# Recurrence computed two tiles at a time inside the input projection, output projection contracted in halves beside the attention norm

## What is computed

```python
proj = h @ W["w_in_even"][e]                      # 2048 -> 5120
q, k, v, xl, gl = jnp.split(proj, [...])          # 1024 columns each
q = rope(rmsnorm(q), pos); k = rope(rmsnorm(k), pos)
o = attn_prompt(q, k, v, lam)  or  attn_sample(q, k, v, k_past, v_past, lam)
o = rmsnorm(o, subln) * (1 - lam_init)            # the attention norm, per head
xc = causal_dwconv(xl, lru_buf, w, b)
r = sigmoid(einsum(xc, wa) + ba); i = sigmoid(einsum(xc, wx) + bx)   # gates, 16 blocks of 64x64
a = exp(-8 * r * softplus(-lam)); drive = sqrt(-expm1(2 log a)) * i * xc
h_t = a_t * h_(t-1) + drive_t                     # the recurrence, over the 1024 channels
yl = gelu(gl) * h
y = concatenate([o, yl]) @ W["w_out_even"][e]     # output projection, 2048 -> 2048
```

## Time and profile before

| | |
|---|---|
| median of 3 runs | 3342.11 us (3337.58 to 3343.0) |
| the profiled execution | 3340.85 us |
| its span, first to last instruction | 3339.1 us |
| TensorE busy | 3139.5 us, 94% of the span |
| VectorE, ScalarE, GpSimd busy | 46%, 32%, 1% |
| mean granted TensorE clock | 0.966 of full speed |
| HBM traffic | 617 MB read, 186 GB/s over the span |

### The profile page before, as it was taken

How to read it: one execution, slowest core, us unless ns; L and a number is a source line. 1 busy time by engine, 2 the same in 40 slices (tenths; PEclk the granted TensorE clock), 3 DMA queues, 4 the chain that set the end, 5 groups by cost and what they waited for, 6 DMA issues and landing times.

```text
span 3339.1 us, 56135 instructions
## 1 busy us (share of the span) xinstructions
PE 3139.5 (94%) x21283; PEld 2863.0 (86%) x21283; DVE 1520.1 (46%) x2024; ACT 1082.2 (32%) x1295; POOL 29.7 (1%) x55
## 2 busy tenths in 40 slices
PE   6899987877899999999999989999899999999998
PEld 2588863447889989989989989999899999999998
DVE  1534565345544433433434554445544444444443
ACT  1322233134333233333233243333343333332332
POOL 0000000100000000000000000000000000000000
PEclk9899997888999999999999989999999999999999
DMA  9777777963476576576566434444444444444443
GB/s 340 246 249 247 252 254 268 340 248 93 147 233 198 159 232 206 158 227 211 160 220 214 151 114 151 147 148 147 126 139 151 150 147 149 150 148 148 150 150 108
DMA packets 512217, 624.17 MB, mean 187 GB/s; under 512 B 22416, under 2 KB 408081, under 8 KB 511444
## 3 DMA queue, kind: packets, MB, share of 16 engines
q1 hardware_dynamic: 504576, 595.68, 55.7%
q0 software_dynamic: 6112, 22.84, 1.8%
q10 hardware_dynamic: 1430, 4.24, 0.4%
HBM read 617.13 MB, written 5.54 MB: 186 GB/s over the span
## 4 chain that ended last, share of the span: by engine, by line
PE 88%; DVE 4%; DMA 4%; ACT 2%; issue 1%; SPq 1%; DVEq 0%; POOL 0%; ACTq 0%; POOLq 0%
PE mm L1452 82%; PE aux L1452 5%; DMA wide_first<-in_ada_mix_w 2%; DMA wide_later<-in_ada_mix_w 2%; PE mm L1545 1%; DVE a_rr L1216 1%; SPq L364 1%; DVE l_g L1336 0%; PE aux L1716 0%; ACT tmp L623 0%; DVE a_qn L1219 0%; DVE p_s L1243 0%; DVE pj L1227 0%; DMA wide_later<-in_ada_mlp_w 0%; DVE rstd L913 0%
## 5 line engine op out<-in xcount | busy, mean ns | idle before, releaser
L859 DVE TENSOR_TENSOR w_lo<-raw,w_hi 128x1024 fp32r<-128x1024 f32 x752 | 919.9, 1225 | 1439.6 <-ACT w_hi L536 1437.9
L536 ACT ACTIVATE w_hi<-raw 128x1024 fp32r<-128x1024 f32 x752 | 795.0, 1058 | 1734.1 <-PE mm L1452 1733.9
L1452 PE MATMUL mm<-h_hi,w_hi 128*128 128x320 f32 x3712 | 1166.0, 314 | 53.0 <-DVE h_lo L955 32.3
L1452 PE MATMUL mm<-h_lo,w_hi 128*128 128x320 f32 x3712 | 1152.4, 310 | 0.0
L1452 PE MATMUL mm<-h_hi,w_lo 128*128 128x320 f32 x3712 | 1152.3, 310 | 0.0
L1452 PEld LDWEIGHTS mm<-h_hi,w_hi 128*128 128x128 f32 x3712 | 702.6, 189 | 145.6 <-issue 145.6
L1452 PE MATMUL mm<-u_hi,w_hi 128*128 128x320 f32 x2304 | 712.0, 309 | 0.0
L1452 PE MATMUL mm<-u_lo,w_hi 128*128 128x320 f32 x2304 | 711.9, 309 | 0.0
L1452 PE MATMUL mm<-u_hi,w_lo 128*128 128x320 f32 x2304 | 711.9, 309 | 0.0
L1452 PEld LDWEIGHTS mm<-h_lo,w_hi 128*128 128x128 f32 x3712 | 702.8, 189 | 0.0
L1452 PEld LDWEIGHTS mm<-h_hi,w_lo 128*128 128x128 f32 x3712 | 702.1, 189 | 0.0
(11 more groups left out here) (256 smaller groups left out, 1241.2 us busy)
## 6 DMA issues: line engine op xcount, KB each, us to landing
raw<-in_mlp_w SPq DMA_DIRECT2D x512, 512.0 KB, 3.6
narrow<-in_ada_mlp_w SPq DMA_DIRECT2D x256, 256.0 KB, 3.5
raw<-in_w_in_odd SPq DMA_DIRECT2D x96, 512.0 KB, 3.6
raw<-in_w_in_even SPq DMA_DIRECT2D x80, 512.0 KB, 6.6
wide_first<-in_ada_mix_w SPq DMA_DIRECT2D x64, 512.0 KB, 8.8
narrow<-in_ada_mix_w SPq DMA_DIRECT2D x128, 256.0 KB, 3.7
wide_later<-in_ada_mlp_w SPq DMA_DIRECT2D x64, 512.0 KB, 6.2
wide_later<-in_ada_mix_w SPq DMA_DIRECT2D x64, 512.0 KB, 10.6
```

The lines of the kernel that those rows point to most:

```text
L536: fn(w_hi[:, slot], raw[:, slot], ACT.Copy).then_inc(hi_ready, 1)
L859: v.tensor_tensor(w_lo[:, slot], raw[:, slot], w_hi[:, slot].bitcast(F32), ALU.subtract).then_inc(lo_ready, 1)
L1452: return nc.tensor.matmul(out, lhsT, rhs, start=first, stop=last)
```

## The change

The recurrence leaves its place ahead of the output projection. It is done two tiles at a time in the turns of the input projection: turn i of the four gets the gate matmuls of tiles 2i and 2i+1 (PE, after the second and the fourth chunk of the second pair), their tanh, exponential and root (ACT), and DVE does the recurrence of pair i in the middle of turn i+1. Convolution and gelu start one turn earlier. The buffers `l_a`, `l_m`, `l_d` hold two tiles instead of eight. The gate weights are loaded at the start. The output projection's first two pairs are computed in halves: both pairs contract first over the recurrence's blocks, with the head sums of the attention norm between those halves, then over the attention's. SP loads the weight chunks in that order, and ACT and DVE interleave the first eight splits with the attention norm.

```diff
-        l_a = at("l_a", RH + LT * TILE, [P, LT, T])
...
+        l_a = at("l_a", RM + 4 * TILE, [P, 2, T])
+        l_m = at("l_m", RM + 6 * TILE, [P, 2, T])
+        l_d = at("l_d", RM + 8 * TILE, [P, 2, T])
         wgate = at("wgate", RU + 16 * TILE, [P, 2, LT, P])
...
             load_quad(slab(W_IN, 0, 11 * COLS))
-            load_quad(slab(A["w_out_even"][0], 0, 0))
+            halves = [slab(A["w_out_even"][0], 0, j * COLS) for j in range(2)]
+            for s in (2, 3):
+                load(halves[0](s))
+            for s in (2, 3):
+                load(halves[1](s))
             sp.wait_ge(chunk_used, 80)
             with looped(sp, 4, GROUPS, {KW: 8}) as g:
                 ada_wide(wide_later, 1, g)
             with looped(sp, 0, 8, {KW: 8}) as g:
                 ada_wide(wide_later, 2, g)
-            matrix(A["w_out_even"][0], 8, 1)
+            for half in halves:
+                for s in (0, 1):
+                    load(half(s))
+            matrix(A["w_out_even"][0], 8, 2)
...
-            turns_with_ada(4)
...
+            turns_with_ada(3)
+            def gates(j):
+                i, m = j // 2, j % 2
+                act.wait_ge(l_gates, j + 1)
+                if i and not m:
+                    act.wait_ge(l_stage, i)
+                fn(l_a[:, m], aux[:, 0, 0:T], ACT.Tanh, scale=0.5, bias=hb[:, 0, j:j + 1])
+                fn(l_d[:, m], mm[:, 2, 0, 0:T], ACT.Tanh, scale=0.5, bias=hb[:, 1, j:j + 1]).then_inc(l_tr, 1)
+                act.wait_ge(l_tr, j + 1)
+                fn(l_m[:, m], l_a[:, m], ACT.Tanh, scale=hb[:, 2, j:j + 1], bias=hb[:, 2, j:j + 1]).then_inc(l_t, 1)
+                act.wait_ge(l_t, 2 * j + 1)
+                fn(l_a[:, m], l_a[:, m], ACT.Exp, scale=hb[:, 3, j:j + 1], bias=hb[:, 3, j:j + 1]).then_inc(l_t, 1)
+                if m:
+                    act.wait_ge(l_t, 2 * j + 2)
+                    fn(l_m[:, :, :], l_m[:, :, :], ACT.Sqrt).then_inc(l_root, 1)
+            for i in range(4):
+                split()
+                act.wait_ge(g_poly, i + 1)
+                fn(g_tmp[:, :, :], g_tmp[:, :, :], ACT.Tanh, scale=GELU_C).then_inc(g_tanh, 1)
+                split(2)
+                gates(2 * i)
+                ada_out()
+                split(2)
+                gates(2 * i + 1)
...
+            act.wait_ge(stored, 64)
+            act.wait_ge(y_val, 4)
+            mixed(2)
+            squared(0)
+            mixed(3)
+            squared(1)
+            act.wait_ge(wide_used, 8 * 24)
+            split(1)
+            rooted(0)
+            split(1)
+            for i in range(1, H):
+                if i + 1 < H:
+                    squared(i + 1)
+                rooted(i)
+                if i in (2, 4):
+                    split(1)
+                if i == 4:
+                    act.wait_ge(s_out, 1)
+                    act.wait_ge(o_ready, 4)
+                    mixed(0)
+            split(2)
+            act.wait_ge(o_ready, H)
             mixed(1)
-            for n in (2, 3):
...
+            split(2)
+            rounds(1)
...
-            def turn_with_ada(out0, out1, a, g, extra=()):
+            def turn_with_ada(out0, out1, a, g, extra=(), mid=None):
                 for n in range(4):
                     split(1)
                     if n < len(extra):
                         extra[n]()
                 out0()
+                if mid is not None:
...
-            def projections(kind, turns, first, group=None, extra=None):
+            starts = slice(SEQ, T, DS)
+            def recurrence(i):
+                for m in range(2):
+                    j = 2 * i + m
+                    dve.wait_ge(l_tr, j + 1)
+                    v.scalar_tensor_tensor(l_d[:, m, 0:SEQ], l_d[:, m, 0:SEQ], 1.0, xl_p[:, j, 3:3 + SEQ], ALU.add, ALU.mult)
+                    d_s = l_d[:, m, SEQ:T].rearrange("p (b q) -> p b q", b=NB)
+                    ins = v.scalar_tensor_tensor(d_s, d_s, 1.0, xl_s[:, j, :, 3:3 + DS], ALU.add, ALU.mult)
+                step(ins)
+                dve.wait_ge(l_t, 4 * i + 4)
+                step(v.tensor_tensor(l_b[:, :, :], l_a[:, :, starts], h0[:, 2 * i:2 * i + 2, :], ALU.mult))
+                dve.wait_ge(l_root, i + 1)
+                step(v.scalar_tensor_tensor(l_m[:, :, :], l_a[:, :, :], 1.0, l_m[:, :, :], ALU.add, ALU.mult))
+                settle()
+                step(v.scalar_tensor_tensor(l_d[:, :, :], l_d[:, :, :], 0.5, l_m[:, :, :], ALU.mult, ALU.mult))
+                step(v.memset(l_a[:, :, starts], 0.0))
+                settle()
+                step(v.tensor_tensor(l_d[:, :, starts], l_d[:, :, starts], l_b[:, :, :], ALU.add))
+                settle()
+                for m in range(2):
+                    ins = v.tensor_tensor_scan(l_m[:, m], l_a[:, m], l_d[:, m], 0.0, ALU.mult, ALU.add)
+                step(ins)
+                settle()
+                y = pj[:, 24 + 2 * i:26 + 2 * i, :]
+                v.scalar_tensor_tensor(y, y, 0.5, l_m[:, :, :], ALU.mult, ALU.mult).then_inc(y_val, 1)
+                v.tensor_copy(lstage[:, 2 * i:2 * i + 2, 27:28], l_m[:, :, SEQ - 1:SEQ])
+                v.tensor_copy(lstage[:, 2 * i:2 * i + 2, 28:36], l_m[:, :, SEQ + DS - 1:T:DS]).then_inc(l_stage, 1)
...
-            projections(project, 4, 4, (1, 0), conv_and_gelu)
+            for i in range(5):
+                a, g = (0, 11) if i == 0 else (1, i - 1)
+                turn_with_ada(lambda: project(0, 4 * i), lambda: project(1, 4 * i + 2), a, g,
+                              conv_and_gelu(i) if i < 4 else (), (lambda: recurrence(i - 1)) if i else None)
...
+            low(2, 1)
+            low(3, 2)
+            split(1)
+            scaled_head(0)
+            split(1)
+            dve.wait_ge(s_back, 1)
+            for n in range(4):
+                rows, cols = slice(4 * (n % 2), 4 * (n % 2) + 4), slice(SEQ + 32 * (n // 2), SEQ + 32 * (n // 2) + 32)
+                ins = v.tensor_scalar(pj[:, rows, cols], mm[:, 2, 0, P * n:P * n + P].rearrange("p (j t) -> p j t", j=4),
+                                      subln[:, 0:1], None, ALU.mult)
+            ins.then_inc(s_out, 1)
+            for i in range(1, H):
+                scaled_head(i)
+                if i in (2, 4):
+                    split(1)
+                if i == 5:
+                    low(0, 3)
+            split(2)
+            low(1, 4)
+            split(2)
+            step(v.memset(sq_sum[:, :, :], 0.0))
...
+            def half_pair(r, s):
+                slot = K.off % SLOTS
+                pe.wait_ge(lo_ready, K.now + 1)
+                pe.wait_ge(h_ready, 4 + (s + 2) % 4 + 1)
+                for kk in range(4):
+                    for m in range(2):
+                        out, cols = mm[:, r, m, 0:T], slice(P * m, P * m + P)
+                        k = 4 * s + kk
+                        mul(out, w_hi[:, slot, kk, cols], h_hi[:, k, :], k == KT // 2, False)
+                        mul(out, w_hi[:, slot, kk, cols], h_lo[:, k, :], False, False)
+                        ins = mul(out, w_lo[:, slot, kk, cols], h_hi[:, k, :], False, k == KT // 2 - 1)
+                ins.then_inc(chunk_used, 1)
+                K.up()
             def norm():
...
+            def gates(j):
+                pe.wait_ge(l_conv, j // 2 + 1)
+                if j:
+                    pe.wait_ge(l_tr, j)
+                for n in range(2):
+                    out = (aux[:, 0], mm[:, 2, 0])[n]
+                    mul(out[:, 0:SEQ], wgate[:, n, j, :], xl_p[:, j, 3:3 + SEQ], True, True)
+                    ins = mul(out[:, SEQ:T].rearrange("p (b q) -> p b q", b=NB), wgate[:, n, j, :],
+                              xl_s[:, j, :, 3:3 + DS], True, True)
+                ins.then_inc(l_gates, 1)
+            pe.wait_ge(gate_in, 64)
+            for i in range(4):
+                def after(s):
+                    if s in (1, 3):
+                        gates(2 * i + s // 2)
+                    if s == 2:
+                        fold()
...
+            def head_sums(*heads):
+                for i in heads:
+                    pe.wait_ge(o_sq, i + 1)
+                    if i >= 2:
+                        pe.wait_ge(o_root, i - 1)
+                    mul((mm[:, 2, 1], aux[:, 0])[i % 2][:, 0:SEQ], C("ones"), l_g[:, 0, i % 2, 0:SEQ], True, True
+                        ).then_inc(o_ms, 1)
+            head_sums(0, 1)
+            pe.wait_ge(pair_free, G.now + 2)
+            half_pair(0, 2)
+            head_sums(2)
+            half_pair(0, 3)
+            head_sums(3)
+            half_pair(1, 2)
+            head_sums(4, 5)
+            half_pair(1, 3)
+            head_sums(6, 7)
+            for r in range(2):
+                half_pair(r, 0)
+                half_pair(r, 1)
+                G.up()
```

161 lines of the change are left out of this document (43 added, 118 removed).

## The result

The changed kernel takes 3301.71 us (median, 3300.98 to 3312.18) where the kernel before took 3339.85 us on the same chip (3336.23 to 3343.0): a ratio of 0.9894, 95% interval 0.9881 to 0.9908. It is 38 us faster (31 to 40 by the interval).

What follows compares the result with a forecast made beforehand. TensorE, busy for 94% of the span, was taken to bound the kernel. From 3340.85 us, 11.7 was added for the projection and 36.2 taken off before the output projection: 3316 us, range 3308 to 3328.

Steps and rivals of the forecast that it cites:

- The projection: Input projection: eight tiles' gate matmuls at 1.46 us each on TensorE's path add 11.7 us (10.6 to 12.8).
- the room before the fold: Input projection: ScalarE's ares copy is done at +13.3, TensorE's fold arrives at +14.3, 1.0 us to spare.
- The stretch before the output projection: Recurrence leaves, norm interleaved with eight splits and half pairs: chunk 8 ends at 774.5 instead of 810.7, saving 36.2 us.
- The clock's share: Output projection's first eight chunks: two slow-clock restarts at 1.5 us and 0.3 for chunk 1.
- waits for sums: Beside the attention norm: 4.8 of VectorE's 34.2 us from 722.9 to 757.1 are waits for head sums.
- rival A: Beside the norm the clock stays low, a chunk costs 6.4 us: 3323.7 (first four) to 3335 (all eight); chance 0.16.
- Nothing elsewhere: After the first eight output-projection chunks: both kernels do the same 24 chunks, so nothing was counted there.
- 810.7 is the time to beat: Output projection: TensorE turns to the row transposes at 810.69 in the old kernel; the new end is compared with it.
- B: Input projection pays more: a tile costs 2.2 us and the fold waits 1 us in three turns: 3325; chance 0.10.
- C: Input projection: recurrence delays gate tile, ares copy and fold; each us beyond 7.3 costs 3, slower than before; chance 0.03.
- D: Output projection: chunk 1 waits until the norm is over, eight chunks end near 774, hardly different; no price of its own.

Runs made afterwards that it cites:

- a_gates_twice: Changed kernel with every gate matmul of the projection done twice, plus 128 empty waits in the opening: 3316.26 us, ratio 0.9932.
- a_scans: Changed kernel with the two scans of each pair of tiles done five times on VectorE: 3328.86 us, ratio 0.9970.
- b_shift34: Kernel before the change, with 34 more empty wait instructions at the start of TensorE's program: 3326.63 us, ratio 0.9958.
- a_shift222: Changed kernel with 222 more empty wait instructions at the start of TensorE's program, putting both MLP bodies where the old kernel has them: 3332.81 us, ratio 0.9979.

## Why the prediction was wrong in size: right in the two terms it priced, wrong in one it put at nothing

- **The projection, +11.7 forecast, +10.1 measured.** A tile costs 1.26 us on average, not 1.46. The one shown takes 1.34, its first function 0.59 where rows 5 have 0.66 and its second 0.75 for 0.80. No fold wait, no PE idle time, as forecast. The recurrence took 5.5 us of VectorE (349.66 to 355.14) for an estimate of 6.3, and the room before the fold was 1.3 for 1.0. a_gates_twice shows the term. a_scans shows the chain, and its waits of 14.8 us for 14.7 bear out the room.
- **The stretch before the output projection, -36.2 forecast, -35.2 measured** (from +10.1 to -25.1). The row transposes were named for 786 and start at 785.5; the pauses before chunks 4 and 5 were named as 3.6 and 5.1 and are 3.58 and 5.76. That the total is right to 1.0 us is partly luck. The clock's share was undersized. Chunk 1 took 5.1 us (738.93 to 744.01), chunk 4 6.2 (756.97 to 763.16), chunks 5 to 8 15.5 for 14.1: 1.6, 2.7 and 1.4 us above full speed, 5.7 in all for the 3.3 forecast. But not all of that is added to VectorE's part, which takes 35.1 us (734.74 to 769.8), 28.7 of work and 6.3 of waits. (The forecast had 33.0 for the same piece, 29.4 and 3.6: the 4.8 us that it called waits for sums include 1.2 for the first h_hi.) The slow chunks 1 and 4 stand ahead of the sums that it waits for, so their loss lies, as the timelines read, for the most part inside those waits. Chunk 5 came 2.2 us later behind the sample part's transposes than in the queues written without the clock (35.3 us for 33.1), chunks 5 to 8 took another 1.4, so 3.6 in all where the forecast had added 3.3. The rule behind rival A, that a burst behind a wait starts on the slow clock (the Trainium skill, "TensorE: Matmul & The Clock Gate", section "HAM oscillation — how this bites in real kernels"), held for chunks 1 and 4, which followed pauses (granted clock 0.50 to 742 and from 756 to 762), and for the start of chunks 5 to 8 (0.50 to 772), and not for chunks 2 and 3, which took 3.7 and 3.6 us at 1.00 with no pause over 0.2 us ahead of them.
- **Nothing elsewhere: this step failed.** The prediction's sentence was that 810.7 is the time to beat, "since after it both kernels do the same 24 chunks". The work is the same, but not its place in the code. The sum put what follows 810.7 at nothing for that reason. It left out -19.6 us in layer 0's MLP and +5.6 in layer 1's, -14.0 in all, and that with the 24.4 makes the 38.7 of the two spans (0.2 us are drift within the blocks). b_shift34 gets the -19.6 with no change to the work at all, a_shift222 takes all of it away from the changed kernel (+20.4 and -5.6 at the joints), and with both bodies placed well the two kernels' medians differ by 24.1 us (19 to 33).
- **What could have been read before.** The six gaps of "issue" in layer 0's MLP were in the trace of the kernel before, with 11.1 us of PE idle time and low clock behind them, and so was q8. A gap whose releaser is "issue" on the engine that bounds a kernel, at the joint of a loop, with instruction packets under it, is a term of any change that alters the length of that engine's program. The sign could not be told without counting instructions; a bound could: about 20 us down if layer 0's gaps went, and as much up, at layer 0's price, if layer 1 got them.
- **Rivals.** A priced the first four chunks at 6.4 us each; of these only chunk 4 (6.2) comes near, and chunk 1 (5.1) half way. B did not. C's chain exists and had 1.3 us of room. D expected chunk 1 behind the norm, and it started beside it; but its reason, that the norm sets the end whatever the interleaving, was close to the truth: without the interleaving the row transposes come 1.5 us later.

What stays open: why b_shift34's layer 1 was fetched again only once (4 us), why the same joint costs 1.8 us in one execution and 4.0 in another, and why the opening's length differs between executions (the first chunk's split starts 2.3 us earlier to 2.2 us later than in the changed kernel's trace in runs that don't touch the opening).

## What to carry to other kernels

Writing out a loop, or adding instructions ahead of one, moves every later loop against the packets in which code is fetched. Here that made a loop body of 1600 to 1800 instructions on TensorE begin or cease to be fetched anew in every turn. Before crediting a change with a gain, compare the same piece of work in both traces stage by stage: a step in code that the change doesn't touch is not the change's. And where several engines share a stage, count the idle time of the one that bounds it between its own instructions; here VectorE bounds, and an order that removed 6.3 us of its idle time was worth 6.4.

## What the runs showed of the hardware

- TensorE kept loop bodies of 1597 and 1767 instructions over four turns at some positions (no packet of q8 from 1100 to 1850 us of the changed kernel) and fetched them again, about nine packets of 16 KB a turn, at others. Moving a program by 34 instructions was worth 12 us of 3339.
- A joint with one stall (1.3 to 2.2 us) cost 1.5 to 4.0 us, one with two stalls 5.9 to 7.2.
- An empty wait on TensorE cost 0.109 us: 222 of them ran from 4.1 to 28.3 us.
- Three pauses of 5 us on TensorE in the projection made 14.8 us of waiting cost 23.3: the granted clock was at 0.50 when work began again and for 5 to 6 us more.
